# The table of relative biases: one row a head, repeated over 128 rows by one transfer, in a one-core decoder kernel

## Chip, cores and metric

One Trainium2 chip, one core. The metric is the device time of one execution in microseconds (us). Three runs of the kernel before gave 2323.56, 2324.03 and 2326.43, median 2324.03.

## The reference, cut to what matters

Two layers of a decoder on 512 tokens and 1024 channels, then a hybrid block with three branches, a gated convolutional MLP and a per-layer embedding. Only the first attention (DSA) and the table that it adds matter here. Everything is float32.

```python
def rel_bucket(dist): ...            # 32 buckets: exact to 15, then logarithmic

proj = h @ w_in                      # 256 c_q, 128 c_kv, 64 k_idx, 8 w_idx
q_idx = einsum('btr,rhd->bthd', c_q, w_q_idx)
rel   = relu(einsum('bqhd,bsd->bqhs', q_idx, k_idx))
score = einsum('bqh,bqhs->bqs', w_idx, rel)      # causal
_, sel = top_k(score, 128)           # the keys that each query may see
logits = einsum('bqhc,bqkc->bqhk', q_abs, c_kv[sel])
logits = logits + rel_bias[rel_bucket(t - sel)]  # one bias a head and distance
p = softmax(logits)
```

The NSA attention of the second layer adds the same biases again.

## The kernel before, in words

The kernel is written engine by engine. Each engine runs one list of instructions in order and waits on counting semaphores: `mark` names a count that an instruction reaches, `wait_ge(*x.when(name))` waits for it. The order is by hand: nothing is moved by a planner. Large products are split in a rounded part and a remainder and take three float32r products (`matmul3`, L538). SP loads the weights in plan order (L490) into a ring of raw buffers as soon as the buffer's last reader is through; ACT rounds a unit (L509), DVE takes the remainder (L520). The one exception is the unit `uq`, whose remainder POOL takes (L1273). PSUM has eight banks that are taken in turn; whoever opens a bank waits for its last reader (L531).

The setup loads, among others, `one_hot` (33 x 640, L922: row = bucket, column = distance, the last row for future keys) and `rel` (33 x 8, L923: the 32 x 8 table, its last row set to -1e30 by DVE at L1202). DSA stage (`dsa_tensor`, `dsa_scalar`, `dsa_vector`, `dsa_pool`):

- PE makes the latents, c_q's norm factors (`sums`, `spread`), then the index queries `q_idx` (L1035) and, for query tiles i = 1, 2, 3 of 128 tokens, eight score products (L1047). ACT applies relu. For i = 1 DVE weighs and adds the heads (L1236, L1239). For i = 2 and 3 ACT weighs them too (L1148, L1150) in two buffers, and POOL adds them (L1264, L1267) and puts the causal mask on (L1269, which marks `score` i). ACT may fill a buffer again only once POOL has added it.
- DVE picks the 128 largest of each row (`choose_keys`, L1194 and L1196, 16 rounds a tile), tile 1, then 2, then 3. For tiles 2 and 3 it waits for POOL's `score`.
- The bias table. ACT spreads `rel` over 128 columns a head (L1126, `rel_wide`). After the scores PE multiplies it with `one_hot`: 8 heads x 2 halves (L1055), each giving 128 equal rows of 320. ACT takes them out of PSUM into four row buffers (L1161), POOL sends each head to `skew` in DRAM ([8, 128, 640], L1277), and at last reads it back with a row step of 639 instead of 640 (L1281), so that row p lands shifted by p: `bias` [128, 8, 512] in SBUF.
- PE turns `uk` (L1063), spreads the kv factors, then makes the queries `uq` (L1076, which waits for POOL's remainder) and absorbs `uk` (L1075); ACT takes both out (L1180, L1171).

Attention stage (`att0_*`): PE needs the last absorbed query before its first logits (L1303, L1309), DVE needs `bias` and the last chosen keys (L1351, L1352) before its first maximum (L819), POOL adds bias and mask into `addends` (L1388) after `bias` and the last `uq` tile (L1379, L1380), ACT rounds a unit of w_o (L517) and loads its table for exp before its first exponential (L827).

The queues around the change: POOL's list has seven sums of squares, scores 2, scores 3, the `uq` remainder, eight sends and the read back, in this order. The transfers of a queue that POOL issues are software transfers; SP's and ACT's are hardware ones.

Of the kernel before, what the change touches and what calls it, by code (L numbers as in the profile page):

```python
# [13 lines left out]
ACT = mybir.ActivationFunctionType  # L14
AX = mybir.AxisListType.X

P = 128
# [4 lines left out]
T = 512  # L22
# [3 lines left out]
HEADS = 8  # L26
# [7 lines left out]
BUCKETS, MAX_DIST = 32, 4096  # L34
N_SHIFT = T + P
# [292 lines left out]
def build_program(nc, a, out):  # L328
    with ExitStack() as ctx:
# [37 lines left out]
        banks = Banks([ctx.enter_context(nc.psum_tensor(f"bank{n}", [P, T], F32)) for n in range(8)])  # L367
        skew = nc.dram_tensor("bias_skew", [HEADS, P, N_SHIFT], F32, kind="Internal")
# [5 lines left out]
        bias = sbuf("bias", P, HEADS, T, scope=bias_scope)  # L374
# [56 lines left out]
        def signal(name):  # L431
            s = Signal(ctx.enter_context(nc.semaphore(name)))
            signals.append(s)
            return s
# [1 line left out]
        const_in, ident_in, hot_in, rel_in, rows_in = (signal(n) for n in ("const_in", "ident_in", "hot_in", "rel_in", "rows_in"))  # L436
        x_in = [signal(f"x_in{n}") for n in range(NT)]
        raw_in = [signal(f"weight_in{n}") for n in range(2 * N_RAW)]
        skew_out = [signal(f"skew_out{n}") for n in range(4)]
        bias_in, misc_in, out_done = signal("bias_in"), signal("misc_in"), signal("out_done")  # L440
        tile_full, rounded, split = signal("tile_full"), signal("weight_rounded"), signal("weight_split")
        (setup, dsa, att0, mlp0, kv, nsa, mlp1, mix, fox, dn, rec, merge, ffn, ple) = (
            Stage(n, signal) for n in ("setup", "dsa", "att0", "mlp0", "kv", "nsa", "mlp1", "mix", "fox", "dn", "rec",
# [87 lines left out]
        def open_bank(pe, name, *freed, hold=False):  # L531

            n, before = banks.take(name, freed, hold)
            for by, what in before:
                pe.wait_ge(*by.when(*what))
            return banks.tensors[n][:, :]
# [119 lines left out]
        def pool_squares(pool, st):  # L656

            for c in range(1, NC):
                pool.wait_ge(*st.act.when("square", c))
                if c > 1:  # L660
                    pool.wait_ge(*st.pool.last())
                pool.e.tensor_tensor(scratch[0], scratch[0], square_buffer(c), ALU.add).then_inc(*st.pool.mark(("part", c)))  # L662
# [93 lines left out]
        def scalar_fold(act, st, name, cols, scale):  # L756
            act.wait_ge(*st.dve.when(name, "folded"))
            act.e.activation(cols, cols, ACT.Sqrt, scale=scale, bias=eps).then_inc(*st.act.mark((name, "root")))
# [218 lines left out]
        key_and_weight = qT_head[0]  # L977
        w_idx = small[:, 700:732]
        best = small[:, 740:748]
        bias_rows = [dsa_step(at, N_SHIFT) for at in (6 * T, 6 * T + N_SHIFT, 0, N_SHIFT)]  # L980
        rel_wide = dsa_step(4 * T, HEADS, P)
        A_IN_TILES = [[(0, P), (P, 2 * P)], [(0, P), (P, 200)]]

        latent_factors = {"cq": small[:, 750:754], "ckv": small[:, 754:758], "kidx": small[:, 732:736]}
        latent_squares = {"cq": relu_bufs, "ckv": [dsa_step(9 * T, T)], "kidx": scores[1:2]}

        def dsa_tensor(pe):
            def sums(name, rows=P):
                bank = open_bank(pe, ("dsa", name, "sums"), (dsa.dve, (name, "folded")), hold=name == "ckv")
                pe.wait_ge(*dsa.act.when(name, "squares"))  # L990
                tensor_token_sums(pe, lambda t: bank[:, t:t + 1], latent_squares[name], ones[:, 0:1], rows
                                  ).then_inc(*dsa.pe.mark((name, "sums")))
# [34 lines left out]
            spread("cq")  # L1027
            latents(2, range(0, 4))
            sums("kidx", 64)
            bank = open_bank(pe, ("dsa", "w_idx"), (dsa.dve, ("w_idx",)))  # L1030
            pe.wait_ge(*dsa.act.when("w_rows"))
            for t in range(NT):
# [6 lines left out]
            for i in range(1, NT):  # L1039
# [4 lines left out]
                for h in range(IDX_HEADS):  # L1044
# [1 line left out]
                    bank = open_bank(pe, ("score", i, h), (dsa.act, ("relu", i, h)))  # L1046
                    pe.e.matmul(bank[:, 0:S], q_idxT[half:half + 64, h // 2, i * P:(i + 1) * P], kidxT[half:half + 64, 0:S],  # L1047
                                start=True, stop=True).then_inc(*dsa.pe.mark(("score", i, h)))
            w = N_SHIFT // 2
            pe.wait_ge(*dsa.act.when("rel_wide"))  # L1050
            pe.wait_ge(*hot_in.when("hot"))
            for h in range(HEADS):
                for half in range(2):
                    bank = open_bank(pe, ("bias", h, half), (dsa.act, ("bias", h, half)))
                    pe.e.matmul(bank[:, 0:w], rel_wide[0:BUCKETS + 1, h, :], one_hot[:, half * w:half * w + w], start=True,  # L1055
                                stop=True).then_inc(*dsa.pe.mark(("bias", h, half)))
            u = unit_at["uk", 0]
            pe.wait_ge(*raw_in[u % (2 * N_RAW)].when("unit", u))
            for half in range(2):
                bank = open_bank(pe, ("ukT", half), (dsa.act, ("ukT", half)))  # L1060
                for n in range(4):
                    h = 4 * half + n
# [23 lines left out]
        def dsa_scalar(act):  # L1086
# [12 lines left out]
            for c in range(2):  # L1099
# [13 lines left out]
            act.e.activation(kidxT[0:64, :], banks.of("latent", 3)[0:64, :], ACT.Copy).then_inc(*dsa.act.mark())  # L1113
            act.e.activation(key_and_weight[64:72, :], banks.of("latent", 3)[64:72, :], ACT.Copy
                             ).then_inc(*dsa.act.mark(("w_rows",), ("kidx", "taken")))
            scalar_fold(act, dsa, "kidx", latent_factors["kidx"], 1.0 / IDX_DIM)
            act.wait_ge(*tile_full.when("q_idx", 0))
            act.e.activation(q_idxT[:, 0, :], banks.of("q_idx", 0), ACT.Copy).then_inc(*dsa.act.mark(("q_idx", 0)))
# [2 lines left out]
            for t in range(1, 4):  # L1121
                act.wait_ge(*tile_full.when("q_idx", t))
                act.e.activation(q_idxT[:, t, :], banks.of("q_idx", t), ACT.Copy).then_inc(*dsa.act.mark(("q_idx", t)))
            act.wait_ge(*dsa.dve.when("neg"))
            act.wait_ge(*rel_in.when("rel"))
            act.e.activation(rel_wide[0:BUCKETS + 1], rel.unsqueeze(2).broadcast_to([BUCKETS + 1, HEADS, P]), ACT.Copy  # L1126
                             ).then_inc(*dsa.act.mark(("rel_wide",)))
            n = 0
            for i in range(1, NT):
                S = (i + 1) * P  # L1130
# [21 lines left out]
                    n += 1  # L1152
            round_upto(act, unit_at["uq", 0])
            scalar_fold(act, dsa, "ckv", latent_factors["ckv"], 1.0 / KV_LORA)
            w = N_SHIFT // 2
            for h in range(HEADS):
                for half in range(2):
                    act.wait_ge(*dsa.pe.when("bias", h, half))
                    if h > 3:
                        act.wait_ge(*skew_out[h % 4].when("skew", h - 4))  # L1160
                    act.e.activation(bias_rows[h % 4][:, half * w:half * w + w], banks.of("bias", h, half)[:, 0:w], ACT.Copy  # L1161
                                     ).then_inc(*dsa.act.mark(("bias", h, half)))
            for half in range(2):
                act.wait_ge(*dsa.pe.when("ukT", half))
                act.wait_ge(*skew_out[1].when("skew", HEADS - 3))
                act.e.activation(w_ukT[:, 4 * half:4 * half + 4, :].rearrange("p h c -> p (h c)"), banks.of("ukT", half), ACT.Copy
                                 ).then_inc(*dsa.act.mark(("ukT", half)))

# [5 lines left out]
            for h in range(HEADS):  # L1174
                if h > 1:
                    keep_q_abs(h - 2)
                else:
                    act.wait_ge(*skew_out[h].when("skew", HEADS - 4 + h))
                act.wait_ge(*tile_full.when("uq", h))
                act.e.activation(qT_head[h % 2], banks.of("uq", h), ACT.Copy).then_inc(*dsa.act.mark(("uq", h)))  # L1180
            keep_q_abs(HEADS - 2)
# [72 lines left out]

        def dsa_pool(pool):
            pool_squares(pool, dsa)
            for i in (2, 3):
                S = (i + 1) * P
                score = scores[i - 1][:, 0:S]
                for h in range(IDX_HEADS):  # L1260
                    n = (i - 1) * IDX_HEADS + h
                    pool.wait_ge(*dsa.act.when("weighted", i, h))
                    if h == 0:
                        pool.e.tensor_copy(score, relu_bufs[n % 2][:, 0:S]).then_inc(*dsa.pool.mark(("added", n)))  # L1264
                    else:
                        pool.wait_ge(*dsa.pool.last())
                        pool.e.tensor_tensor(score, score, relu_bufs[n % 2][:, 0:S], ALU.add).then_inc(*dsa.pool.mark(("added", n)))  # L1267
                pool.wait_ge(*dsa.pool.last())
                pool.e.tensor_tensor(score[:, S - P:S], score[:, S - P:S], causal[:, T - P:T], ALU.add  # L1269
                                     ).then_inc(*dsa.pool.mark(("score", i)))  # L1270
            uq = unit_at["uq", 0]
            pool.wait_ge(*rounded.when("unit", uq))
            pool.e.tensor_tensor(split_flat(uq, 1), raw_flat(uq), f32(split_flat(uq, 0)), ALU.subtract  # L1273
                                 ).then_inc(*dsa.pool.mark(("unit", uq)))
            for h in range(HEADS):
                pool.wait_ge(*dsa.act.when("bias", h, 1))
                pool.e.dma_start(skew[h], bias_rows[h % 4]).then_inc(*skew_out[h % 4].mark(("skew", h), by=16))  # L1277
            sheared = bass.AP(tensor=skew, offset=P - 1, ap=[[N_SHIFT - 1, P], [P * N_SHIFT, HEADS], [1, T]])
            for n in range(4):
                pool.wait_ge(*skew_out[n].when("skew", HEADS - 4 + n))  # L1280
            pool.e.dma_start(bias[:, :, :], sheared).then_inc(*bias_in.mark(("bias",), by=16))  # L1281


        att_dsa = Attention(att0, dsa_soft, 0)
# [1838 lines left out]
```

## Time and profile before

| | us |
|---|---|
| median of 3 runs (lowest to highest) | 2324.03 (2323.56 to 2326.43) |
| span of the profiled execution, first to last instruction | 2320.8 |
| time of the profiled execution beside its span | not given apart; the median is 3.2 above the span |
| PE busy in the span | 2278.3 (98%) |
| DSA stage, latents to chosen keys | about 17 to 125 in the span |
| first attention | about 125 to 180 |

The profile lists, for one execution, how long each engine was busy, which chain of waits ended last, and where each transfer landed. An average over the span says little about the DSA stage, which takes 5% of it, so that stage is read by its own windows and timelines. "PEclk" or the granted clock is 1.00 at 2.4 GHz and 0.50 at 1.2 GHz.

### The profile page before, as it was taken

The page shows a single profiled execution, that of the slowest core. Times are in us where ns is not written, and L with a number is a line of the kernel's source. Part 1 is how long each engine was busy: PE and PEld are TensorE (multiplying, and loading weights), DVE is VectorE, ACT ScalarE, POOL GpSimd, SP SyncE. Part 2 cuts the span into 40 slices and gives each one's busy share as a digit, 9 for nine tenths or more (in the row PEclk, how much of TensorE's full clock was granted, in tenths as well). Part 3 has the DMA queues.
Part 4 walks back from the last instruction along what each step waited for, and adds up shares of the span by engine and source line. Part 5 has one row for each costly group of instructions (what it writes and reads, how often), then busy time and mean ns, then how long its engine had stood idle before and what let it go on. Part 6 is the DMA issues. An engine that isn't in the chain of part 4 may idle for free.

```text
span 2320.8 us, 26065 instructions
## 1 busy us (share of the span) xinstructions
PE 2278.3 (98%) x10840; PEld 1847.8 (80%) x10840; DVE 1128.2 (49%) x1726; ACT 869.6 (37%) x1289; POOL 390.0 (17%) x339
## 2 busy tenths in 40 slices
PE   7999999999999999999999999999999999999998
PEld 5567888888876678888888978888888888888887
DVE  4974433434324645343345576554333446555453
ACT  5674222223223643122134386442322244233243
POOL 1431110112200002011022303332101211000020
PEclk9799999999999999999999999999999999999999
DMA  4203322322251012322336622224355333332331
GB/s 138 100 1 109 109 91 91 108 92 91 96 166 61 1 57 92 106 91 91 109 83 85 56 34 58 55 37 73 73 91 96 98 96 91 106 94 91 99 106 59
DMA packets 221955, 196.26 MB, mean 85 GB/s; under 512 B 7264, under 2 KB 215596, under 8 KB 221709
## 3 DMA queue, kind: packets, MB, share of 16 engines
q1 hardware_dynamic: 219820, 188.92, 31.2%
q0 software_dynamic: 1504, 5.51, 0.7%
q8 instruction: 85, 1.39, 0.3%
q14 instruction: 33, 0.27, 0.0%
q10 hardware_dynamic: 513, 0.17, 0.0%
HBM read 189.87 MB, written 4.72 MB: 84 GB/s over the span
## 4 chain that ended last, share of the span: by engine, by line
PE 89%; DVE 6%; ACT 3%; issue 1%; DMA 0%; ACTq 0%; POOL 0%; DVEq 0%; POOLq 0%
PE bank L540 24%; PE bank L542 24%; PE bank L541 24%; PE bank L2210 5%; PE bank L863 2%; PE bank L2396 2%; DVE dsa_latents L1196 1%; PE bank L1679 1%; PE bank L1506 1%; DVE small L1194 1%; PE bank L714 1%; PE bank L724 1%; PE bank L847 1%; ACT hybrid_step L827 1%; PE bank L1309 1%; DVE weight_lo L526 1%
## 5 line engine op out<-in xcount | busy, mean ns | idle before, releaser
L540 PE MATMUL bank<-h_hi,weight_hi 128*128 128x512 f32 (+1 forms) x1568 | 615.5, 393 | 4.7 <-DVE h_lo L646 3.6
L542 PE MATMUL bank<-h_hi,weight_lo 128*128 128x512 f32 (+1 forms) x1568 | 611.6, 390 | 0.0
L541 PE MATMUL bank<-h_lo,weight_hi 128*128 128x512 f32 (+1 forms) x1568 | 611.1, 390 | 0.0
L526 DVE TENSOR_TENSOR weight_lo<-weight_raw,weight_hi 128x2048 fp32r<-128x2048 f32 (+3 forms) x181 | 382.9, 2116 | 375.6 <-ACT weight_hi L517 375.6
L517 ACT ACTIVATE weight_hi<-weight_raw 128x2048 fp32r<-128x2048 f32 (+2 forms) x182 | 319.8, 1758 | 341.6 <-PE bank L542 312.9
L540 PEld LDWEIGHTS bank<-h_hi,weight_hi 128*128 128x128 f32 (+1 forms) x1568 | 294.2, 188 | 68.6 <-issue 7.4
L542 PEld LDWEIGHTS bank<-h_hi,weight_lo 128*128 128x128 f32 (+1 forms) x1568 | 294.0, 188 | 63.4
L541 PEld LDWEIGHTS bank<-h_lo,weight_hi 128*128 128x128 f32 (+1 forms) x1568 | 294.3, 188 | 61.5 <-issue 0.2
L540 PE MATMUL bank<-hidden_hi,weight_hi 128*128 128x512 f32 x512 | 201.8, 394 | 0.0
L542 PE MATMUL bank<-hidden_hi,weight_lo 128*128 128x512 f32 x512 | 200.7, 392 | 0.0
L541 PE MATMUL bank<-hidden_lo,weight_hi 128*128 128x512 f32 x512 | 198.7, 388 | 0.0
L633 DVE TENSOR_TENSOR xT<-bank,xT 128x512 f32<-128x512 f32 x112 | 77.1, 690 | 224.0 <-PE bank L542 224.0
L1457 POOL TENSOR_TENSOR mlp_room<-mlp_room 128x512 f32<-128x512 f32 x64 | 86.1, 1348 | 524.5 <-DVE mlp_room L1437 524.5
L1413 ACT ACTIVATE hidden_hi<-mlp_room 128x512 fp32r<-128x512 f32 x64 | 40.5, 633 | 245.5 <-POOL mlp_room L1457 245.5
L662 POOL TENSOR_TENSOR norm_scratch<-norm_scratch 128x512 f32<-128x512 f32 x42 | 57.2, 1362 | 444.9 <-ACT norm_scratch L654 424.3
L542 PEld LDWEIGHTS bank<-hidden_hi,weight_lo 128*128 128x128 f32 x512 | 96.1, 188 | 22.5
L541 PEld LDWEIGHTS bank<-hidden_lo,weight_hi 128*128 128x128 f32 x512 | 96.1, 188 | 21.5
L540 PEld LDWEIGHTS bank<-hidden_hi,weight_hi 128*128 128x128 f32 x512 | 96.3, 188 | 19.2
L1437 DVE SCALAR_TENSOR_TENSOR mlp_room<-bank,norm_scratch 128x512 f32<-128x512 f32 x64 | 43.9, 689 | 101.5 <-PE bank L542 95.7
L2210 PE MATMUL bank<-h_hi,weight_hi 128*128 128x512 f32 x208 | 83.7, 402 | 0.9 <-DVE weight_lo L526 0.9
L2210 PE MATMUL bank<-h_hi,weight_lo 128*128 128x512 f32 x208 | 83.1, 400 | 0.0
L2210 PE MATMUL bank<-h_lo,weight_hi 128*128 128x512 f32 x208 | 82.8, 398 | 0.0
(412 smaller groups left out, 3159.4 us busy)
## 6 DMA issues: line engine op xcount, KB each, us to landing
weight_raw<-in_w_down SPq DMA_DIRECT2D x40, 1024.0 KB, 5.1
weight_raw<-in_w_up SPq DMA_DIRECT2D x32, 1024.0 KB, 5.4
weight_raw<-in_w_up SPq DMA_DIRECT2D x44, 512.0 KB, 5.1
weight_raw<-in_w_in SPq DMA_DIRECT2D x20, 1024.0 KB, 9.0
weight_raw<-in_w_in SPq DMA_DIRECT2D x24, 512.0 KB, 6.8
weight_raw<-in_w_kv_shared SPq DMA_DIRECT2D x6, 1024.0 KB, 4.9
weight_raw<-in_w_branch SPq DMA_DIRECT2D x6, 1024.0 KB, 5.0
weight_raw<-in_a_w_o SPq DMA_DIRECT2D x4, 1024.0 KB, 6.0
```

What stands on the lines that cost most here:

```text
L517: act.e.activation(split_flat(v, 0), raw_flat(v), ACT.Copy).then_inc(*rounded.mark(("unit", v)))
L526: dve.e.tensor_tensor(split_flat(v, 1), raw_flat(v), f32(split_flat(v, 0)), ALU.subtract).then_inc(*split.mark(("unit", v)))
L540: pe.e.matmul(o, w[0], x[0], start=start, stop=False)
L541: pe.e.matmul(o, w[0], x[1], start=False, stop=False)
L542: return pe.e.matmul(o, w[1], x[0], start=False, stop=stop)
L633: dve.e.tensor_tensor(xT[:, tile, :], banks.of(*name, tile), xT[:, tile, :], ALU.add).then_inc(*st.dve.mark(name + (tile,), ("x", tile)))
L662: pool.e.tensor_tensor(scratch[0], scratch[0], square_buffer(c), ALU.add).then_inc(*st.pool.mark(("part", c)))
L863: done = pe.e.matmul(bank[:, n * P:T], value_tile(n), self.turned[j % 2][:, n, n * P:T], start=first and n == 0, stop=last and n == NT - 1)
L1437: dve.e.scalar_tensor_tensor(squares[n % 2], banks.of("up", layer, s, c), 0.0, rstd, ALU.max, ALU.mult).then_inc(*st.dve.mark(("relu", s, c)))
L1457: pool.e.tensor_tensor(buf, buf, buf, ALU.mult).then_inc(*st.pool.mark(("squared", s, c)))
L2210: done = pe.e.matmul(banks.of(*item), w[part == 2], x[part == 1], start=i == 0, stop=i == 23)
L2396: done = pe.e.matmul(bank[:, tiles[t]], lhs(t), rhs(t), start=True, stop=True)
```

## The change

The table is made as one row a head. PE multiplies `rel` (33 x 8) itself with the two halves of `one_hot`: 2 products into 8 rows of a bank, right after the sums for the index key. ACT takes them out (2 x [8 x 320]) into `bias_row`. POOL sends `bias_row` (8 partitions x 640) with a zero step over 128 rows into all of `skew` by one transfer, before the sums of scores 2, and reads it back after scores 2, before scores 3, where it waits for the first transfer. `rel_wide`, the 16 products, their 16 copies and the 8 sends go, and so do ACT's waits for the sends.

```diff
-        skew_out = [signal(f"skew_out{n}") for n in range(4)]
-        bias_in, misc_in, out_done = signal("bias_in"), signal("misc_in"), signal("out_done")
+        skew_out, bias_in, misc_in, out_done = (signal(n) for n in ("skew_out", "bias_in", "misc_in", "out_done"))
...
-        bias_rows = [dsa_step(at, N_SHIFT) for at in (6 * T, 6 * T + N_SHIFT, 0, N_SHIFT)]
-        rel_wide = dsa_step(4 * T, HEADS, P)
+        bias_row = dsa_step(4 * T, N_SHIFT)
...
+        BIAS_PARTS = [(0, N_SHIFT // 2), (N_SHIFT // 2, N_SHIFT)]
...
             sums("kidx", 64)
+            pe.wait_ge(*hot_in.when("hot"))
+            pe.wait_ge(*rel_in.when("rel"))
+            pe.wait_ge(*dsa.dve.when("neg"))
+            for n, (c0, c1) in enumerate(BIAS_PARTS):
+                bank = open_bank(pe, ("bias", n), (dsa.act, ("bias", n)))
+                pe.e.matmul(bank[0:HEADS, 0:c1 - c0], rel, one_hot[:, c0:c1], start=True, stop=True
+                            ).then_inc(*dsa.pe.mark(("bias", n)))
             bank = open_bank(pe, ("dsa", "w_idx"), (dsa.dve, ("w_idx",)))
...
-            w = N_SHIFT // 2
-            pe.wait_ge(*dsa.act.when("rel_wide"))
-            pe.wait_ge(*hot_in.when("hot"))
-            for h in range(HEADS):
-                for half in range(2):
-                    bank = open_bank(pe, ("bias", h, half), (dsa.act, ("bias", h, half)))
-                    pe.e.matmul(bank[:, 0:w], rel_wide[0:BUCKETS + 1, h, :], one_hot[:, half * w:half * w + w], start=True,
-                                stop=True).then_inc(*dsa.pe.mark(("bias", h, half)))
             u = unit_at["uk", 0]
...
                              ).then_inc(*dsa.act.mark(("w_rows",), ("kidx", "taken")))
+            for n, (c0, c1) in enumerate(BIAS_PARTS):
+                act.wait_ge(*dsa.pe.when("bias", n))
+                act.e.activation(bias_row[0:HEADS, c0:c1], banks.of("bias", n)[0:HEADS, 0:c1 - c0], ACT.Copy
+                                 ).then_inc(*dsa.act.mark(("bias", n)))
             scalar_fold(act, dsa, "kidx", latent_factors["kidx"], 1.0 / IDX_DIM)
...
-            act.wait_ge(*dsa.dve.when("neg"))
-            act.wait_ge(*rel_in.when("rel"))
-            act.e.activation(rel_wide[0:BUCKETS + 1], rel.unsqueeze(2).broadcast_to([BUCKETS + 1, HEADS, P]), ACT.Copy
-                             ).then_inc(*dsa.act.mark(("rel_wide",)))
...
-            for h in range(HEADS):
-                for half in range(2):
-                    act.wait_ge(*dsa.pe.when("bias", h, half))
-                    if h > 3:
-                        act.wait_ge(*skew_out[h % 4].when("skew", h - 4))
-                    act.e.activation(bias_rows[h % 4][:, half * w:half * w + w], banks.of("bias", h, half)[:, 0:w], ACT.Copy
-                                     ).then_inc(*dsa.act.mark(("bias", h, half)))
             for half in range(2):
                 act.wait_ge(*dsa.pe.when("ukT", half))
-                act.wait_ge(*skew_out[1].when("skew", HEADS - 3))
...
                     keep_q_abs(h - 2)
-                else:
-                    act.wait_ge(*skew_out[h].when("skew", HEADS - 4 + h))
...
         def dsa_pool(pool):
             pool_squares(pool, dsa)
+            for n in range(2):
+                pool.wait_ge(*dsa.act.when("bias", n))
+            pool.e.dma_start(skew[:, :, :], bias_row[0:HEADS].unsqueeze(1).broadcast_to([HEADS, P, N_SHIFT])
+                             ).then_inc(*skew_out.mark(("skew",), by=16))
             for i in (2, 3):
...
+                if i == 2:
+                    sheared = bass.AP(tensor=skew, offset=P - 1, ap=[[N_SHIFT - 1, P], [P * N_SHIFT, HEADS], [1, T]])
+                    pool.wait_ge(*skew_out.when("skew"))
+                    pool.e.dma_start(bias[:, :, :], sheared).then_inc(*bias_in.mark(("bias",), by=16))
             uq = unit_at["uq", 0]
...
-            for h in range(HEADS):
-                pool.wait_ge(*dsa.act.when("bias", h, 1))
-                pool.e.dma_start(skew[h], bias_rows[h % 4]).then_inc(*skew_out[h % 4].mark(("skew", h), by=16))
-            sheared = bass.AP(tensor=skew, offset=P - 1, ap=[[N_SHIFT - 1, P], [P * N_SHIFT, HEADS], [1, T]])
-            for n in range(4):
-                pool.wait_ge(*skew_out[n].when("skew", HEADS - 4 + n))
-            pool.e.dma_start(bias[:, :, :], sheared).then_inc(*bias_in.mark(("bias",), by=16))
```

## Rows read from the trace of the kernel before

**Rows 1.** The page: span, busy time of each engine.
```profile
span 2320.8 us, 26065 instructions
PE 2278.3 (98%) x10840; PEld 1847.8 (80%) x10840; DVE 1128.2 (49%) x1726; ACT 869.6 (37%) x1289; POOL 390.0 (17%) x339
```

**Rows 2.** Chain of waits, 50 to 62 us: start, us, what.
```profile
54.41 0.60 ACT dsa_latents L1123
55.00 0.94 ACT dsa_latents L1126
55.94 0.28 ACT dsa_latents L1141
56.24 0.36 DVE dsa_latents L1236
```

**Rows 3.** The same chain from 98 us on.
```profile
99.76 0.70 DVE small L1194
...
124.70 0.44 DVE dsa_kept L1198
...
128.26 0.82 ACT dsa_softmax L827 x2
...
129.87 2.37 PE bank L847 x10
132.23 3.81 PE bank L1309 x8
...
138.19 1.09 PE bank L847 x10
139.28 2.16 PE bank L1309 x8
```

**Rows 4.** Timeline of PE: start, us, what; in brackets idle time before.
```profile
47.37 0.38 PE L1033 MATMUL bank<-const,dsa_latents 8*128 8x8 f32 x4 [0.23 <-DVE small L752]
55.05 2.00 PE L1047 MATMUL bank<-dsa_kept,dsa_latents 64*128 64x256 f32 x16 [0.69 <-ACT dsa_latents L1123]
101.39 0.80 PE L540 MATMUL bank<-cq_hi,weight_hi 128*128 128x512 f32 x1 [1.25 <-ACT dsa_latents L1166]
121.90 4.58 PE L1309 MATMUL bank<-dsa_kept 128*128 128x128 f32 x16 [0.25 <-ACT dsa_kept L1171]
```

**Rows 5.** Timeline of ACT around the stage's end.
```profile
121.25 0.60 ACT L1171 ACTIVATE dsa_kept<-bank 128x512 f32<-128x512 f32 x1 [0.35 <-PE bank L1075]
122.22 1.91 ACT L517 ACTIVATE weight_hi<-weight_raw 128x2048 fp32r<-128x2048 f32 x1
124.15 1.28 ACT L827 ACT_TABLE_LOAD   x1
...
127.00 0.19 ACT L827 ACTIVATION_READ_ACCUMULATOR dsa_softmax<-dsa_softmax,softmax_statistics 128x1 f32 x1
```

**Rows 6.** Timeline of POOL.
```profile
73.36 0.61 POOL L1264 COPY dsa_latents<-dsa_latents 128x512 f32<-128x512 f32 x1
74.48 9.74 POOL L1267 TENSOR_TENSOR dsa_latents<-dsa_latents 128x512 f32<-128x512 f32 x7 [0.50 <-ACT dsa_latents L1150]
84.72 4.53 POOL L1273 TENSOR_TENSOR weight_lo<-weight_raw,weight_hi 128x2048 fp32r<-128x2048 f32 x1
102.81 0.91 POOL L1281 DMA_DIRECT2D bias<-bias_skew  x1 [3.01 <-DVE dsa_latents L1196]
```

**Rows 7.** Windows: us, busy (count) of each engine, granted clock, DMA share, GB/s.
```profile
36.00:38.00 2.00, 2.00 (x12) 1.33 (x10) 0.00 (x0) 0.00 (x0) 0.00 (x0) 1.00 1.03 422
130.00:136.00 6.00, 6.00 (x19) 4.41 (x20) 5.04 (x20) 4.02 (x15) 2.96 (x4) 0.55 0.00 0
```

**Rows 8.** DMA issues in the window 88 to 120: count, KB each, median us to landing.
```profile
bias_skew<-dsa_latents POOLq DMA_DIRECT2D x8, 320.0 KB, 4.3
bias<-bias_skew POOLq DMA_DIRECT2D x1, 2048.0 KB, 10.2
```

**Rows 9.** Groups by line and shape, 60 to 126 us: busy, mean ns, idle before.
```profile
L1055 PE MATMUL bank<-small,dsa_latents 33*128 33x320 f32 x32 | 20.0, 779 | 2.8 <-ACT dsa_latents L1161 2.6
L1161 ACT ACTIVATE dsa_latents<-bank 128x320 f32<-128x320 f32 x16 | 5.8, 441 | 8.5 <-DMA bias_skew<-dsa_latents 8.4
```

More of the change, by code:

```diff
@@ L1154, in dsa_scalar @@
             scalar_fold(act, dsa, "ckv", latent_factors["ckv"], 1.0 / KV_LORA)
-            w = N_SHIFT // 2
-            for h in range(HEADS):
-                for half in range(2):
-                    act.wait_ge(*dsa.pe.when("bias", h, half))
-                    if h > 3:
-                        act.wait_ge(*skew_out[h % 4].when("skew", h - 4))
-                    act.e.activation(bias_rows[h % 4][:, half * w:half * w + w], banks.of("bias", h, half)[:, 0:w], ACT.Copy
-                                     ).then_inc(*dsa.act.mark(("bias", h, half)))
             for half in range(2):
                 act.wait_ge(*dsa.pe.when("ukT", half))
-                act.wait_ge(*skew_out[1].when("skew", HEADS - 3))
                 act.e.activation(w_ukT[:, 4 * half:4 * half + 4, :].rearrange("p h c -> p (h c)"), banks.of("ukT", half), ACT.Copy
```

## The prediction

> **What bounds the kernel now.** I read the page first [rows 1]: PE is busy 98% of 2320.8 us, so outside the start every us of PE counts. The DSA stage is the exception, and only the chain of waits shows it. At 54.41 the last index query is copied by ACT, then ACT spreads the bias table (L1126, 0.94), and from 56.24 on the chain is DVE alone [rows 2]: 48 rounds of choosing keys, the last 16 from 99.76 to 125.14 [rows 3]. Then the first softmax, and from 129.87 PE again. So PE's and ACT's bias work between 73 and 101, 32 passes with 20.0 us busy and 16 copies of 5.8 us with 8.5 us of waits [rows 9], lies beside DVE's chain. Removing it buys nothing by itself: PE and ACT only reach the end of the stage earlier, and wait there for DVE. Last, I read POOL's timeline, since the change puts a wait into POOL's list, and scores 3, which DVE needs at 99.76, are behind it [rows 3, 6].
>
> **The start of DVE's chain.** Removed: L1126, 0.94 us between the last query copy and the first relu [rows 2]. Added ahead of it on PE: two products of 320 columns. Eight passes over 1280 columns (four tile widths) take 2.16 us at full clock [rows 3], 1.69 ns a column, so 0.54 each, 1.08 together. PE idles 0.23 just there [rows 4], so the queries come 0.85 late: last copy ends at 55.85. The first score product then needs its own time, no longer covered by L1126: it starts 0.05 after the copy [rows 2, 4], takes 256 x 1.69 ns = 0.43 and some 0.3 to release ACT, so relu starts at 56.65 where it started at 55.94. DVE's chain starts 0.7 late. ACT's two new copies (0.44 each by L1161's mean [rows 9]) end at about 48.95 and push the key's root; PE wants that factor one query tile later, at 50.0, and gets it about 49.7: nothing, and if the cover fails, some tenths. The two new banks were last used by latents long read: nothing. The loads that PE now waits for were issued in the setup, over 30 us earlier: nothing.
>
> **The transfer that repeats the rows.** POOL issues it at about 49.0 (an issue of this kind costs 0.91 [rows 6]; POOL is idle there, its next work comes at about 64). It writes 8 x 128 x 640 x 4 B = 2.62 MB, read from eight partitions. No row shows a large transfer from so few. Bounds: at the rate of 128 partitions, 422 GB/s [rows 7], 6.2 us. If the rate goes with the partitions read, 16 engines carry 26.4 GB/s each for 8 partitions each, and 8 rows get one engine's share: 99 us. I take twice that share, 52.8 GB/s and **49.7 us**: nearer to the width end, since the only thing in which this transfer differs from the 422 row is its width. Overhead: the send of 320 KB needed 4.3 us of which 0.8 are bytes, the read back 10.2 of which 5.0 are [rows 8]; I take 3. It lands at L = 49.0 + 3 + 49.7 = 101.7.
>
> The Trainium skill (SBUF — State Buffer, Door 1: The DMA port swizzle) says that four neighbouring partitions share one DMA port, and gives 27.6 GB/s for partitions 0 to 3 and 104 for 0 to 15. By it eight rows have two ports, 54 GB/s, and the transfer takes 48 us, the sum ending 1.5 lower. No row here shows it.
>
> **What waits for it.** POOL ends scores 2 and meets the wait at 73.4 [rows 6], 28 us too early. Behind it in POOL's list:
> - issue of the read back 0.95; scores 3, which took 73.36 to 84.72 with 0.50 of idling [rows 6], 10.9. DVE gets them at L + 11.85 = 113.5 instead of being served at 99.76 without waiting. DVE's last 16 rounds take 25.4 [rows 3]: L + 37.3.
> - ACT's weighing for tile 3 has two buffers that POOL empties, so ACT stops after two heads and resumes with POOL; its rounding of uq ends with scores 3 as before. POOL's remainder of uq, 4.53 [rows 6]: L + 16.4. PE's uq product starts at L + 16.5 instead of 101.39 [rows 4]; from its start to the last absorbed query's copy it took 121.85 - 101.39 = 20.46 [rows 4, 5]: L + 37.0.
> - Then on ACT, in order, the token copy, rounding of w_o and the table for exp, until 125.43, 3.58 after that copy [rows 5]; the first three exponentials, until 127.2 [rows 5], 1.75; the fourth 0.82 [rows 3]. L + 37.0 + 3.6 + 1.75 + 0.8 = L + 43.1, where it was 129.08 [rows 3]. DVE is ahead: from the chosen keys to the fourth maximum it took 3.1 (125.14 to 128.26 [rows 3]), so L + 40.4, or a us more if it meets PE's logits, which start at L + 37.0.
>
> With L = 101.7 the first transposes move by 101.7 + 43.1 - 129.1 = 15.7 us. Before, PE idled 3.4 before them (the logits end at 126.5 [rows 4]) and ran them and the next logits at half clock: 2.37 and 3.81, against 1.09 and 2.16 once at full [rows 3], the granted clock being 0.55 over 130 to 136 [rows 7]. Now the logits end at L + 41.6 and PE idles about 2, so up to 2.9 may come back; I take half, -1.5. The read back lands at L + 11, long before use. After the attention PE is the bound as before. Sum: 15.7 - 1.5 = **+14.2**, span 2335.0. The median is 3.2 above the span of the profiled run; carried over: **2338**.
>
> The wait decides nothing as long as L + 11.85 is before DVE's own 100.45 (with the 0.7) and L + 43.1 before 129.8: L up to about 87, some 35 us for the bytes, 75 GB/s. Above that each us of L is one us of time.
>
> **Rivals.**
> - **Not slower: the eight rows are read fast enough.** For it: eight engines, one a row, at 26.4 each [rows 7] make 211 GB/s, 12.4 us; even 40% of that lands in time. Against: nothing in the trace except the width. L = 64, POOL never waits, the read back starts at 73.4 and lands at 84. What is left is the start, +0.7, and PE idles longer before the first transposes, which ran at half clock before too [rows 3]: nothing. 2324.7, between 2322.5 and 2327.
> - The Trainium skill (DMA: Bandwidth & Descriptors, How many engines) says that the slowest dimension of both sides sets the number of DMA engines, here eight. Alone it would give this rival, not the forecast.
> - **All eight rows behind one engine's share.** 99 us, L = 151.3: everything from scores 3 on goes 50 us further, about 2388. For it: the arithmetic of 128 rows over 16 engines. Against: one engine's share needs all eight rows to sit in one engine's group.
> - **Faster by more than 0.2%.** The transfer is quick, and PE, ACT and POOL, free of the bias work 20 us earlier, shorten the path into the attention: 0.94 from L1126 without the delay on PE, and 2.9 of half clock; together -3.8, still under 0.2%. It takes something that I do not see, such as a choosing of keys that runs quicker beside an idle machine.
> - The change does what it says: 8 + 1 transfers become 2 and the products 2. I see no case in which it doesn't.
>
> **How the numbers follow.** 0.2% is 4.6 us, about what a measurement of this kernel can tell from no change. The forecast's case, with 45 to 54 us for the bytes and the clock regained or not: 2332 to 2343, chance 0.58. One share: 0.04. In between (L of 87 to 95): 0.04, of which half is slower. In time: 0.29. Faster beyond 0.2%: 0.05. Slower 0.58 + 0.04 + 0.02 = 0.64, within 0.2% 0.31, faster 0.05. The range must hold both main cases: 2323 to 2343. The likeliest case's own is 2332 to 2343.
>
> **What the profile after would show.** The first transfer's time to landing, about 53 us; POOL idle 28 us before the read back, released by that transfer; DVE idle about 13 us before its last 16 rounds, released by POOL; ACT idle in tile 3's weighing; uq's product at about 118; first exponential at about 142. The copy of 8 x 320 on ACT twice near 48.5, the first relu at 56.6. I'm wrong if the first transfer lands in under 35 us (then the time stays at 2324 to 2325), or if with a late landing DVE doesn't wait.

## The result, and the profile after

The changed kernel takes **2356.15 us** (median of 4 runs, 2354.53 to 2358.01) beside 2323.8 of the kernel before: ratio 1.0132, 95% interval 1.0121 to 1.0144. It is slower by 32.4 us. The forecast was 2338, with a range of 2323 to 2343. The direction was right and so was the cause, POOL's wait; the size was not (14.2 of the 32.4 us were forecast), nor the place where DVE stops. The kernel before varies: beside the experiments its medians over 15 to 25 runs were 2325.7 to 2326.5, and against those the changed kernel is about 30 us slower.

The page of the changed kernel, to be read beside [rows 1]: 35 us more span, 12 us less work on PE.

```profile
span 2355.9 us, 25979 instructions
PE 2266.7 (96%) x10812; PEld 1844.0 (78%) x10812; DVE 1130.4 (48%) x1726; ACT 863.9 (37%) x1274; POOL 387.4 (16%) x332
```

Its DMA issues between 44 and 180 us (count, KB each, us to landing), which answer to [rows 8]:

```profile
bias_skew<-dsa_latents POOLq DMA_DIRECT2D x1, 2560.0 KB, 54.4
bias<-bias_skew POOLq DMA_DIRECT2D x1, 2048.0 KB, 8.9
```

The one transfer of 2.62 MB needs 54.4 us. The eight sends of the same bytes needed some 4.3 each and partly overlapped: the first was issued at 89.18, and the read back, which waits for all of them, at 102.81 [rows 6]. The windows of the changed kernel (us, busy and count of PE, PEld, DVE, ACT, POOL, granted clock, DMA share, GB/s) show its rate, and what the engines do meanwhile:

```profile
70.00:80.00 10.00, 8.10 (x15) 2.61 (x14) 9.24 (x32) 6.76 (x12) 5.32 (x6) 0.64 0.50 52
80.00:90.00 10.00, 0.00 (x0) 0.00 (x0) 9.44 (x24) 0.00 (x0) 0.00 (x0) 0.50 0.49 51
90.00:100.00 10.00, 0.00 (x0) 0.00 (x0) 0.01 (x1) 0.00 (x0) 0.00 (x0) 0.50 0.48 50
100.00:110.00 10.00, 1.12 (x4) 0.72 (x4) 0.00 (x0) 3.77 (x6) 5.20 (x5) 0.50 0.55 140
```

50 GB/s, at a mean busy share of 0.5 of the 16 DMA engines. From 80 on only DVE works, from 90 to 100 no compute engine at all. The waits of that stretch (who waited for whom: us in total, times, longest) give the order:

```profile
ACT dsa_latents L1147 <- POOL dsa_latents L1256: 29.0, 1, 29.0
...
POOL bias L1266 <- DMA bias_skew<-dsa_latents: 28.3, 1, 28.3
DVE small L761 <- ACT small L757: 27.9, 2, 26.4
```

POOL stands 28.3 us before the read back, ACT 29.0 for POOL's sums, and DVE 26.4 for a root on ACT. DVE's own timeline shows where (last rounds of the first half of tile 2, then the stop):

```profile
89.47 0.54 DVE L1184 MATCH_REPLACE8 dsa_latents<-small,dsa_latents 128x384 f32<-128x384 f32 x1
116.43 0.18 DVE L761 RECIPROCAL small<-small 128x4 f32<-128x4 f32 x1 [26.42 <-ACT small L757]
116.64 4.15 DVE L763 TENSOR_TENSOR small<-small 128x4 f32<-128x4 f32 x1
120.83 0.56 DVE L1182 MAX8 small<-dsa_latents 128x8 f32<-128x384 f32 x1
```

It is not the start of tile 3's rounds, as forecast, but the middle of tile 2's. There DVE takes the reciprocal of the kv latent's root (`vector_unfold("ckv")` inside `choose_keys(2)`). ACT makes this root (L757; L758 before) only after all of tile 3's heads and the rounding of `uq`. On ACT:

```profile
76.28 0.72 ACT L1149 ACTIVATE dsa_latents<-dsa_latents,small 128x512 f32<-128x512 f32 x1
106.01 0.60 ACT L1147 ACTIVATE dsa_latents<-bank 128x512 f32<-128x512 f32 x1 [29.01 <-POOL dsa_latents L1256]
...
114.32 1.89 ACT L516 ACTIVATE weight_hi<-weight_raw 128x2048 fp32r<-128x2048 f32 x1
116.12 0.28 ACT L757 ACTIVATE small<-small,const 128x4 f32<-128x4 f32 x1
```

The first transposes and logits of the attention, on the chain of waits:

```profile
161.40 2.37 PE bank L846 x10
163.76 2.85 PE bank L1298 x8
```

The tally from the start of DVE's chain to the first transposes closes within 0.2 us. The transposes start at 161.40 instead of 129.87 [rows 3]: 31.5 us. DVE's chain starts at 58.81 instead of 56.24 [rows 2]: 2.6. The stop is 26.4. The tiny product behind it takes 4.15 where it took 0.48, 3.7 more; another such product at 79.8 takes 0.16 where it took 1.18, since POOL stands, 1.0 less. 2.6 + 26.4 + 3.7 - 1.0 = 31.7.

Through the rest of the program the distance to the kernel before stays at 30.55 us until about 1400, by the times at which SP issues the weights. In the profiled execution it is then 31.9 at 1657 and 35.1 from 1709 on. In between PE has two stretches at a lower granted clock in the hybrid block, 0.91 from 1420 to 1440 and 0.83 from 1680 to 1700. A window of the first:

```profile
1430.00:1450.00 20.00, 19.08 (x96) 0.91 0.23 58
```

where the trace before shows 1.00 at the same work. The spans of the four runs differ (2352.6 to 2355.9). So about 2 of the 32.4 us lie there, where the change alters no instruction; that they are chance is likely, not shown.

### The profile page after: what moved, and what is told of

The parts are those of the page before. It is cut to its first block, busy times and chain, and to the rows that moved or that the text cites. A ratio compares the mean times of both kernels' runs of the same rounds, so it can differ in the third digit from the quotient of the medians.

```text
span 2355.9 us, 25979 instructions
## 1 busy us (share of the span) xinstructions
PE 2266.7 (96%) x10812; PEld 1844.0 (78%) x10812; DVE 1130.4 (48%) x1726; ACT 863.9 (37%) x1274; POOL 387.4 (16%) x332
## 4 chain that ended last, share of the span: by engine, by line
PE 90%; DVE 5%; ACT 3%; another core or an unknown queue 1%; issue 0%; DMA 0%; POOL 0%; SPq 0%; ACTq 0%; DVEq 0%; POOLq 0%
PE bank L539 24%; PE bank L541 23%; PE bank L540 23%; PE bank L2199 5%; PE bank L862 3%; PE bank L2385 2%; PE bank L1668 1%; PE bank L1495 1%; PE bank L846 1%; PE bank L713 1%; PE bank L723 1%; PE bank L2075 1%; DVE dsa_latents L1184 1%; DVE small L1182 1%; PE bank L1298 1%
```

## The experiments

All change the changed kernel; none leaves out work. A "stop" is the idle time at POOL's wait for the first transfer.

### The wait last in POOL's list

```diff
-                if i == 2:   # wait for skew_out, read bias back, before scores 3
...
+            (the same three lines, behind the uq remainder)
```

> The changed kernel with POOL's wait for the first transfer and the read back moved behind the uq remainder, last in POOL's list; the narrow transfer itself stays. If the wait's place in POOL's list is the cause, POOL, ACT and DVE no longer stop at 76: the transfer still takes about 54 us and lands near 104, the table lands near 114, before DVE wants it at 127. Left is the late start of DVE's chain, 58.4 instead of 55.9, so 2.5 us: 2326 (2324 to 2329). Rival, the narrow transfer hurts in another way (it starves the other queues, or the eight products cost the time): then it stays above 2340.

Measured: 2325.08 us (2323.95 to 2328.82) beside 2325.7, ratio 1.0001 (0.9991 to 1.001). The transfer is as slow as before, but nobody stands behind it; the read back goes out at 104.6 and lands by 115. Its DMA issues:

```profile
bias_skew<-dsa_latents POOLq DMA_DIRECT2D x1, 2560.0 KB, 54.5
bias<-bias_skew POOLq DMA_DIRECT2D x1, 2048.0 KB, 10.1
```

So the place of the wait makes 31 of the 32 us. What the slow transfer and the earlier products cost by themselves is too little for the time to tell; in the trace the first transposes come at 131.01, 1.1 us later than before.

### The root ahead of ACT's stop

```diff
                 for h in range(IDX_HEADS):
+                    if i == 3 and h == 2:
+                        scalar_fold(act, dsa, "ckv", latent_factors["ckv"], 1.0 / KV_LORA)
...
             round_upto(act, unit_at["uq", 0])
-            scalar_fold(act, dsa, "ckv", latent_factors["ckv"], 1.0 / KV_LORA)
```

> The changed kernel with one instruction moved: ACT takes the root of the kv factor before the third head of tile 3 instead of after the whole tile and the rounding of uq. Theory: DVE's stop halfway through tile 2's rounds (26.4 us until 116.4, then 4.15 us in one tiny product beside POOL's uq remainder) comes only from this root being queued behind ACT's stop. With it early, DVE ends tile 2 near 101 and stops for scores 3 until 116, as the prediction had it: tile 3's rounds end near 141.5 and the first transposes come near 148 instead of 161.4. 2343 (2340 to 2346). Rival: the two stops add nothing to each other and PE's uq product sets the end: then less than 4 us are gained, 2352 to 2356.

Measured: 2341.73 us (2 runs), ratio 1.0069 (1.0049 to 1.0089): 14.4 us less than the changed kernel. The middle of tile 2 passes without a stop, and DVE now stands where the prediction had put it, before tile 3's rounds:

```profile
116.42 0.69 DVE L1183 MAX8 small<-dsa_latents 128x8 f32<-128x512 f32 x1 [15.64 <-POOL dsa_latents L1262]
```

The chain of this kernel, at the first transposes and logits:

```profile
148.09 2.30 PE bank L846 x10
```

148.1 against 161.4. The rival, that the two stops add nothing to each other, falls: 13.3 us of the delay are the root's place. They count the tiny product behind the root too, which takes 0.16 us here, at 90.23, where it took 4.15.

### The eight rows apart

```diff
+        rel_rows = dsa_step(4 * T + N_SHIFT, 32)      # ACT: each head's column four times
...
-                pe.e.matmul(bank[0:HEADS, 0:c1 - c0], rel, one_hot[:, c0:c1], start=True, stop=True
+                pe.e.matmul(bank[0:32, 0:c1 - c0], rel_rows[0:BUCKETS + 1], one_hot[:, c0:c1], start=True, stop=True
...
-            pool.e.dma_start(skew[:, :, :], bias_row[0:HEADS].unsqueeze(1).broadcast_to([HEADS, P, N_SHIFT])
+            pool.e.dma_start(skew[:, :, :], bias_row[0:32:4].unsqueeze(1).broadcast_to([HEADS, P, N_SHIFT])
```

> The changed kernel, but the eight source rows lie in partitions 0, 4, 8 to 28 instead of 0 to 7 (PE makes 32 rows, four equal ones a head; ACT spreads the table over 32 columns in an idle stretch). Same bytes, same eight rows, same zero step, same queue and place. If neighbouring partitions share a way out, the rate grows with the groups of four, eight instead of two: 54.4 us to landing become 14 to 18, POOL does not wait at 76, and the time is 2326 (2324 to 2329). If it is the number of rows, of DMA engines or the zero step that sets 50 GB/s, it stays at 54 us and 2356.

Measured: 2327.97 us (2323.55 to 2329.37), ratio 1.0005 (0.9995 to 1.0016). The transfer takes

```profile
bias_skew<-dsa_latents POOLq DMA_DIRECT2D x1, 2560.0 KB, 15.1
```

and runs at this rate (window as above):

```profile
54.00:58.00 4.00, 3.31 (x18) 2.47 (x18) 0.00 (x0) 1.78 (x3) 0.00 (x0) 1.00 0.51 211
```

Same bytes, same eight rows, same repetition, the same busy share of the DMA engines (0.51 against 0.48 to 0.50): 211 GB/s instead of 50. What sets the 50 is which partitions the rows lie in, not how many rows or DMA engines there are.

### 128 rows, and 16

```diff
+            repeated = skew[:, :, :].rearrange("h (r j) n -> (h r) j n", r=16)      # r=2 for 16 rows
+            pool.e.dma_start(repeated, bias_row[0:128].unsqueeze(1).broadcast_to([128, P // 16, N_SHIFT])
```

> The changed kernel, but with 16 equal rows a head in all 128 partitions, each sent 8 times by the one transfer of 2.62 MB at the same place. Both theories of the rate expect full width here: 8 to 14 us to landing, POOL free at 76, the read back lands near 86. 2326 (2324 to 2328), the late start of DVE's chain being left; if PE's clock no longer falls near 49 us, 2324.5.

Measured: 2325.42 us (2323.79 to 2326.76) beside 2325.7, ratio 1.0 (0.999 to 1.0009).

> The changed kernel, but with two equal rows a head in partitions 0 to 15, each sent 64 times by the one transfer. Neighbouring partitions share a way out in groups of four at some 26 GB/s a group: four groups give 105 GB/s, 25 us for the bytes and 27 to 29 to landing, near 77 to 79, so POOL waits 1 to 3 us at 76, which ACT and DVE hardly see: 2326 (2324 to 2330). If the number of DMA engines set the rate (eight rows, eight engines), 16 rows give full width as e4 had it, 9 us. If each row had its own limit of 6.6 GB/s (8 rows at 50), this gives 105 too, but e3's 8 rows at 210 already speak against that.

Measured: 2328.75 us (2327.27 to 2329.59) beside 2326.19, ratio 1.0014 (1.0003 to 1.0024), at the edge of what can be told. To landing, first with 128 rows, then with 16:

```profile
bias_skew<-dsa_latents POOLq DMA_DIRECT2D x1, 2560.0 KB, 8.9
```

```profile
bias_skew<-dsa_latents POOLq DMA_DIRECT2D x1, 2560.0 KB, 28.2
```

Rates, in the same order (the first two rows for 128 rows). The transfer of the 128 rows ends within the second of its windows, so the first shows its pace:

```profile
52.00:54.00 2.00, 2.00 (x10) 1.65 (x9) 0.00 (x0) 1.24 (x3) 0.00 (x0) 1.00 1.01 389
54.00:58.00 4.00, 3.31 (x23) 2.29 (x22) 1.02 (x3) 2.03 (x6) 0.00 (x0) 1.00 0.87 333
```

```profile
54.00:58.00 4.00, 3.31 (x20) 2.50 (x20) 0.00 (x0) 1.70 (x5) 0.00 (x0) 1.00 0.97 100
```

With 16 neighbouring rows all DMA engines are in use (0.97) and still only 100 GB/s pass, so their number does not set it either. Eight neighbouring partitions 50, sixteen 100, eight of which each is four from the next 211: about 25 to 26 GB/s for each group of four neighbours.

The size of the group is not shown by these runs. Groups of eight neighbours at 50 to 53 GB/s give the same three rates, and neither four neighbouring rows nor rows eight apart were tried. That it is four is what the Trainium skill (SBUF — State Buffer, Door 1: The DMA port swizzle) states: four neighbouring partitions share a DMA port, with asymptotes of 109 GB/s for four ports and 218 for eight; for two ports its 27.2 a port gives an estimate of 54. The measured 100, 211 and 50, read from SBUF, agree. Its rule on the number of DMA engines (DMA: Bandwidth & Descriptors, How many engines), eight for an outermost dimension of eight, agrees with the busy shares (0.5 with eight rows, 0.97 with 16); it does not set the 50 GB/s. At 211 GB/s ports and engines are eight each, so which of them ends that rate stays open.

The 16 rows also show how thin the cover is. POOL waits only 2.08 us, yet the first transposes come at 134.42, 4.55 us after those of the kernel before. POOL's and DVE's timelines:

```profile
77.37 0.93 POOL L1271 DMA_DIRECT2D bias<-bias_skew  x1 [2.08 <-DMA bias_skew<-dsa_latents]
89.30 4.51 POOL L1274 TENSOR_TENSOR weight_lo<-weight_raw,weight_hi 128x2048 fp32r<-128x2048 f32 x1
```

```profile
90.34 0.17 DVE L761 RECIPROCAL small<-small 128x4 f32<-128x4 f32 x1
90.55 3.27 DVE L763 TENSOR_TENSOR small<-small 128x4 f32<-128x4 f32 x1
```

DVE does not wait for the root: ACT has it at 89.41. Of the 4.55 us, 1.8 are the late start of DVE's chain (58.07 against 56.24), and 2.8 are the tiny product, which took 0.48 before. Two sections on, e7 shows what holds it.

### The narrow transfer from SP's queue

```diff
-            (POOL's wait for the copies and its dma_start)
+                if u == unit_at["uv", 0]:      # in SP's list, behind the load of uv
+                    (wait for both copies)
+                    sp.e.dma_start(skew[:, :, :], bias_row[0:HEADS].unsqueeze(1).broadcast_to([HEADS, P, N_SHIFT])
```

> The changed kernel, but SP issues the narrow transfer (a hardware queue) instead of POOL. The way out of the eight partitions is the same: 50 to 56 us to landing, the stops of POOL, ACT and DVE stay, 2354 to 2358. If it is POOL's software queue with its 1024 rows to write that sets the pace, it lands much sooner and the time falls to 2326.

Measured: 2354.24 us (2 runs), ratio 1.0123 (1.0104 to 1.0143). Issued at 48.67, and POOL's wait ends at 102.8:

```profile
102.83 1.05 POOL L1262 DMA_DIRECT2D bias<-bias_skew  x1 [28.72 <-DMA bias_skew<-dsa_latents]
```

54 us again, at 51 GB/s from 50 to 54 us. The kind of queue plays no part here.

### The products later, with 128 rows

The two products go behind `latents(2, ...)` in tile 2's turn, the copies behind ACT's copy of the kv latent; the rest is the kernel with 128 rows.

> The kernel with 128 rows (e4), and the two products with their copies moved behind the scores of tile 1, out of the path to DVE's first round. The products cost PE time where it waits for ACT anyway. DVE's chain then starts where it did before the change or 0.2 to 0.3 us sooner, since the spread of the table that stood there is gone, instead of 1.1 to 2.5 later; scores 2 come up to 1 us later, within the 4 us that DVE leaves them. Expected 2323.5 to 2325 beside 2324 to 2326 of the kernel before: no difference that can be measured, and no way to see a gain, since DVE's rounds set the stage's end. Rival: PE and ACT, free 20 us earlier, shorten the start of the attention: 2320 to 2322.

Measured: 2324.43 us (2323.2 to 2328.06) beside 2326.19, ratio 0.9997 (0.9988 to 1.0006). DVE's chain starts at 55.59, 0.65 before [rows 2], but the first transposes come at 130.23, 0.36 later than before: a us is lost on the way. DVE's and POOL's timelines of this kernel show it, the tiny product that follows the root, and POOL's remainder of uq:

```profile
87.58 0.17 DVE L761 RECIPROCAL small<-small 128x4 f32<-128x4 f32 x1
87.78 1.87 DVE L763 TENSOR_TENSOR small<-small 128x4 f32<-128x4 f32 x1
```

```profile
85.12 4.51 POOL L1274 TENSOR_TENSOR weight_lo<-weight_raw,weight_hi 128x2048 fp32r<-128x2048 f32 x1
```

87.78 + 1.87 = 89.65, and 85.12 + 4.51 = 89.63. The product ends with POOL's instruction. So it does in the changed kernel (116.64 + 4.15 = 120.79, POOL's 116.29 + 4.50 = 120.79) and with 16 rows (90.55 + 3.27 = 93.82, POOL's 89.30 + 4.51 = 93.81). In the kernel before it did so too, but began late enough to lose little: 88.79 + 0.48 = 89.27, POOL's 84.72 + 4.53 = 89.25.

### The tiny product after POOL's remainder

The edit is against the kernel of e7; `choose_keys` takes the round as an argument.

```diff
-            choose_keys(dve, 2, lambda: vector_unfold(dve, dsa, "ckv", latent_factors["ckv"], roots))
+            choose_keys(dve, 2, lambda: vector_unfold(dve, dsa, "ckv", latent_factors["ckv"], roots), 10)   # was 8
```

> The kernel with the products later (e7), and DVE's reciprocal and tiny product of the kv factor two rounds further on in tile 2 (before round 11 instead of 9). In four traces that product ended with POOL's uq remainder, to 0.02 us, however late it began: 1.87 us in e7, 3.27 with 16 rows, 4.15 in the changed kernel, for work that takes 0.16 when POOL idles. Theory: DVE cannot read two SBUF operands while POOL's instruction runs. Begun at about 90.1, after POOL's remainder has ended at 89.6, it takes 0.16 to 0.2, and the first transposes come 1.7 us sooner than e7's 130.23, near 128.6. Time 2322 to 2324 beside 2324 to 2326 of the kernel before, so at best at the edge of what can be told. Rival: the tiny product is slow for another reason (it waits for the semaphore of the reciprocal or of ACT): it stays over 1.5 us and the transposes stay at 130.

Measured: 2322.59 us (2322.01 to 2325.34) beside 2326.52, ratio **0.9988** (0.9979 to 0.9997). DVE, and POOL's remainder, which has ended at 89.79:

```profile
90.24 0.17 DVE L761 RECIPROCAL small<-small 128x4 f32<-128x4 f32 x1
90.44 0.16 DVE L763 TENSOR_TENSOR small<-small 128x4 f32<-128x4 f32 x1
```

```profile
85.27 4.52 POOL L1274 TENSOR_TENSOR weight_lo<-weight_raw,weight_hi 128x2048 fp32r<-128x2048 f32 x1
```

The first transposes start at 128.71, 1.5 sooner than with the products merely later and 1.2 sooner than before the change. This is the one version clear of the kernel before, by 0.1%. The trace of this stage shows 1.2 us of it, the medians differ by 3.9. The granted clocks of the runs tell the two apart: eight of the 15 runs of the kernel before had a mean clock of 0.988 and took 2326.5 to 2328.3 us; the other seven (0.989 and 0.990) have a median of 2323.84, 1.25 above this version, of whose 11 runs none was below 0.990. Whether the version keeps such executions away, or they missed it by chance, is not shown.

## Why the prediction was wrong

**What bounds the stage: right.** DVE's rounds set its end. In e1 the bias work is gone from PE and ACT, and the time is that of before, 2325.08 against 2325.7.

**The transfer: right within 5%.** The sum took 52.8 GB/s and landing at 101.7. Measured were 50 GB/s, 54.4 us and POOL's release at 104.4. That is 2.7 us late, us for us in the time. The choice between 6.2 and 99 us, for the end that goes by width, held; the reason behind it (one engine's share for eight partitions, taken twice) was not the right one: what counts is the groups of neighbours in which the rows lie, with the number of DMA engines unchanged (e3). So the size of this term came out by luck. The rival that eight engines read the rows fast enough fell.

**What waits for it: here it failed.** The step was "DVE gets them at L + 11.85 = 113.5 instead of being served at 99.76 without waiting. DVE's last 16 rounds take 25.4". It followed ACT's stop only into the rounding of uq and PE's product, and left out the instruction right behind that rounding on ACT, the kv root, for which DVE waits in the middle of tile 2. So 8 rounds of tile 2 (10 us), which the sum had run in the shadow of the transfer, came after it too, and with them the tiny product that stood beside POOL's remainder (4.15 us). e2, with the root alone moved ahead, brings the forecast chain: the same stop before tile 3, and first transposes at 148.09, where the working with the measured landing gives 104.4 + 43.1, the exponential's end, and 0.8 on to the transposes, 148.3.

The price of the missing link is 161.4 - 148.1 = 13.3 us of the 18.2 by which the forecast missed the time; the late landing is 2.7. The rest is about what the clock took: some 2 in the hybrid block, and 0.5 that did not come back at the attention.

**The point from which the wait decides** was put at L of about 87. It lies near 76, where POOL meets the wait: POOL's remainder of uq ends 16.4 us after its release, and the tiny product on DVE stands until then. In e5 POOL is released at 77.4 and the product takes 3.27 us. The root itself is late only from about 78 on (an estimate: DVE wants it at 90.3 there, and ACT has it 12.0 after POOL's release).

**The start of DVE's chain** was put at +0.7 and measured +2.6. The products cost nearly what was reckoned, 1.18 us against 1.08 (e1, 47.34 to 48.52). That trace, at full clock, has 57.38, +1.1; PE was 0.28 late in it already at the sums before the products. In the changed kernel PE's granted clock also fell to 1.2 GHz, half of full speed, from about 49 to 52 us (0.75 over 48 to 50, 0.50 over 50 to 52), right behind the sums and the small products; its chain starts 1.4 later than that of e1. The traces of e2, e3 and e5 show the same fall, those of e1, e4 and e6 do not; why is open.

**The clock at the attention**: forecast were 1.5 us back out of 2.9; the first transposes and logits take 2.37 and 2.85, so 1.0 came back.

**Faster by more than 0.2%** did not happen in any version; the best is 0.12% under.

## What to carry to other kernels

A wait moved into an in-order queue is priced by following every instruction behind it to its readers, on every engine that stops in turn, and down to the smallest one: here a root of 128 x 4 values behind ACT's stop held up the engine that set the pace for 26 us. A transfer that repeats a few rows reads them through the few partitions that they lie in, so place the sources apart or make enough copies with the product that makes them anyway (the two products kept PE busy for 1.32 us with 128 columns of `rel` and for 1.24 with 8), and put the wait for it where its engine has nothing else to do.

## What the runs showed of the hardware

- The rate at which a DMA reads SBUF goes by which partitions it reads: 50 GB/s from partitions 0 to 7 (51 from SP's queue), 100 from 0 to 15, 211 from 0, 4, 8 to 28, 389 from all. Groups of four neighbours at 25 to 26 each fit, and so would groups of eight at 50 to 53.
- A DVE instruction with two operands in SBUF stands until a running POOL instruction has ended: 128 x 4 elements took 0.16 us beside an idle POOL and 1.87, 3.27 and 4.15 beside its 4.5 us instruction, which has its operands in SBUF too, ending within 0.02 us of it. DVE's rounds of choosing keys ran at their pace meanwhile (in the kernel before, its search for the eight largest of 128 x 384 took 0.56 us from 80 to 84, beside POOL's sums, and from 85 to 88, beside its remainder, as it did in the changed kernel beside an idle POOL). The Trainium skill (SBUF — State Buffer, SBUF: two separate sides) states such a lock between the two engines; the traces agree.
